# A two-layer decoder trunk on one core: the router's stage in quarters of a tile, the last expert batch in halves

## The chip, the cores and the metric

One Trainium2 chip, one of its cores. The metric is device time in microseconds (us) of one execution, lower is better. Everything is float32. The engines are PE (TensorE), DVE (VectorE), ACT (ScalarE), POOL (GpSimd) and SP (SyncE, which here only issues DMAs); each runs its own instructions in order, and they meet in semaphores.

## What is computed

Two layers (`DEPTH`), 256 tokens, width 1024. Each layer has a token mixer (three kinds of attention over one input projection, then one output projection) and a mixture of experts, each followed by a LayerNorm over `ALPHA * x + sublayer(x)`. The part that the change touches, cut from the reference:

```python
o = jnp.concatenate([o_a, o_b, o_c], axis=1).transpose(0, 2, 1, 3).reshape(B, S, MIX_W)
return o @ w_out                       # the mixer's output projection
# then x = layer_norm(ALPHA * x + that)

s = jax.nn.sigmoid((xf @ router_w).astype(jnp.float32))      # 64 experts in 8 groups
sb = (s + router_b).reshape(T, N_GROUPS, EXP_PER_GROUP)
g_sel = jnp.argmax(lax.top_k(sb, 2)[0].sum(-1), axis=-1)     # top-1 group
_, j = lax.top_k(in_grp, TOP_K)                              # top-2 experts of it
# for each block of tokens of an expert e, with its gates:
hb = jax.nn.silu(xb @ w1[e]) * (xb @ w3[e])                  # 1024 -> 256
return hb @ w2[e]                                            # 256 -> 1024
```

All 64 experts of a layer are read, 3 MiB each (`w1`, `w3`, `w2`), 192 MiB in a layer.

## The kernel before, in words

Tokens stand in two tiles of 128 (t = 0, 1). A layer runs in three stages.

**Mixer.** SP streams `w_in`, PE projects, attends pair by pair, and ends with `out_chunk(t, h, c)` (line 672): tile t, column half h (512 columns), chunk c of 8. Eight chunks make a half of a tile; `mix_psum` counts the halves.

**Router stage.** DVE's `add_mix(t, h)` (line 1141) adds the residual into x and takes the statistics; PE turns the result chunk by chunk (`transpose_z`, line 570), ACT copies it to `xT`, PE multiplies by the router (`route`, line 794; `z_psum`), DVE computes the scores and the choice (`scores`, `select`, lines 1174 and 1189; `picked`), PE counts ranks (`rank`), DVE places (`place`, line 1215), and PE gathers the first batch's rows (`gather_first`, line 840) in two banks. DVE scales its first four chunks into `xg` (line 1277), ACT the other four (line 1513). While this runs the normalised rows x are finished: tile 0 by DVE (`center_first`, then `stretch`, `x0_ready`), tile 1 by POOL in four instructions (lines 519 and 523, `x1_ready`), which start when `routed` is up. PE's order is written out by hand in lines 810 to 862, DVE's in 1244 to 1282, ACT's in 1500 to 1515.

**Experts in batches.** A batch is four experts (k = 0 to 3) of 32 rows each, 16 batches in a round. `batch` (line 876) multiplies `w1` and `w3` (line 890, `part_psum` once for each k), folds four partial sums (897), has DVE compute silu times up (1304 to 1307) from ACT's exponential, turns the hidden rows (912), copies them to `hT` (DVE, 1311), multiplies by `w2` (`down`, line 919; `y2_psum`) and adds the rows to Y (927). Before its k = 2 product PE waits for DVE's copy of k = 0 (line 885), and DVE reaches that copy (1294) only after all of its router stage, `start_batches` (line 1282, a load of the batch count into a register) and `choose`. Between the projections of a batch PE gathers the rows of the next (871).

**Weights.** There are two sets of slots, even and odd. The two first batches are loaded during the mixer. SP issues batch 2's `w1` and `w3` of expert k when batch 0's `part_psum` k is up (`load_first`, line 415), then, when x0 and x1 are ready, one matrix that is still missing of batch 1 (`load_w2(1, 3, 1)`, line 430), then batch 2's four `w2` when batch 0's `y2_psum` is up (431). All later ones follow the same rule, two batches back. The last batch's `w2` come as eight column halves: four first halves (`w2_first_in`), then four second ones (448 to 453). In the last batch the first halves are multiplied for all k (932), the second ones k by k (937); `keep_warm` products fill some waits.

Of the kernel before, what the change touches and what calls it, by code (L numbers as in the profile page):

```python
# [79 lines left out]
def program(nc, a, consts, const_at, out):  # L80
# [17 lines left out]
    with ctx:  # L98
# [129 lines left out]
        class Signal:  # L228
# [23 lines left out]
        xT_psum, xT_dve, xT_act = Signal("xT_psum", 8), Signal("xT_dve", 3), Signal("xT_act", 7)  # L252
# [10 lines left out]
        mix_psum = Signal("mix_psum", 4)  # L263
# [5 lines left out]
            Signal("z_ready", 4), Signal("n_ready", 2), Signal("y_bits_set", 4), Signal("y_seeded", 4))  # L269
# [4 lines left out]
        chosen_ok, xg_dve, xg_act = Signal("chosen_ok"), Signal("xg_dve"), Signal("xg_act")  # L274
        gathered = Signal("gathered_first_half"), Signal("gathered_second_half")
# [9 lines left out]
        w2_first_in = Signal("w2_last_first_half_in", NB * 16)  # L285

        shift_ok, n2_ready = Signal("n2_shift_ok", 2), Signal("n2_ready", 4)
        out_dve, out_pool = Signal("out_dve"), Signal("out_pool")
        y2_first, y_half = Signal("y2_last_first_half_psum", 1), Signal("y_first_half_added", 2)
# [33 lines left out]
        def _(sp):  # L323
# [3 lines left out]
            for l in range(DEPTH):  # L327
# [27 lines left out]
                if l == 0:  # L355
# [26 lines left out]
                sp.dma_start(router.rearrange("p (h c) e -> p h (c e)", h=2),  # L382
                             a["router_w"].rearrange("(h p c) e -> p h (c e)", h=2, c=4)).then_inc(router_in.sem, 16)
                sp.dma_start(router_bias, a["router_b"].partition_broadcast(P)).then_inc(router_in.sem, 16)
                for v, name in enumerate(("ln1_g", "ln1_b")):
                    sp.dma_start(g_cols[:, v, :], a[name].rearrange("l (p c) -> l p c", c=DC)[l]).then_inc(cols_in.sem, 16)
                    sp.dma_start(r_cols[:, v, :].rearrange("p (h c) -> p h c", h=2),
                                 a[name].rearrange("l (h p c) -> l p h c", h=2, c=4)[l]).then_inc(cols_in.sem, 16)
# [19 lines left out]
                after(sp, l, mix_psum, 4)  # L408
# [57 lines left out]
        def _(pool):  # L466
# [5 lines left out]
            for l in range(DEPTH):  # L472
# [40 lines left out]
                after(pool, l, xT_psum, 8)  # L513
# [24 lines left out]
        def _(pe):  # L538
# [16 lines left out]
            for l in range(DEPTH):  # L555
# [14 lines left out]
                def transpose_z(t, h):  # L570

                    after(pe, l, z_ready, 2 * t + h + 1)
                    zc = x[:, t, h * 512:(h + 1) * 512].rearrange("p (d c) -> p c d", c=4)
                    for c in range(4):
                        last = nc.tensor.transpose(bank[2 * t + h][:, c * P:(c + 1) * P], zc[:, c, :], ident)
                    last.then_inc(xT_psum.sem, 1)

# [216 lines left out]
                def route(t, h):  # L794
                    after(pe, l, xT_act, 3 + 2 * t + h + 1)
                    if t == 1 and h == 0:
                        after(pe, l, z_lin, 1)
                    for c in range(4 * h, 4 * h + 4):
                        last = mm(bank[0][:, t * NE:(t + 1) * NE], xT[:, c, t * P:(t + 1) * P], router[:, c, :],
                                  start=c == 0, stop=c == DC - 1)  # L800
                    if h == 1:
# [10 lines left out]
                transpose_z(0, 0)  # L812
                transpose_z(0, 1)
# [16 lines left out]
                out_chunk(1, 1, 5)  # L830
                out_chunk(1, 1, 6)
                out_chunk(1, 1, 7)
                route(1, 0)
                set_bits(0, 0)
                transpose_z(1, 1)

                set_bits(0, 1)
                route(1, 1)

                def gather_first(t):  # L840
                    nc_ = nrm[t].rearrange("p (d c) -> p c d", c=DC)
                    for c in range(DC):
                        last = mm(bank[2 + c // 4][:, c % 4 * P:(c % 4 + 1) * P], nc_[:, c, :], chosen[:, t, :],
                                  start=t == 0 and c % 4 == 0, stop=t == 1, skip_group_check=True)
                        if t == 1 and c % 4 == 3:
                            last.then_inc(gathered[c // 4].sem, 1)
# [29 lines left out]
                def batch(j, parity, last_of_all):  # L876
# [32 lines left out]
                    pe.wait_ge(hn_ok.sem, b + 1)  # L909
                    hc = hn.rearrange("p (f c) -> p c f", c=2)  # L910
                    for c in range(2):
                        last = nc.tensor.transpose(bank[1][:, SEQ + c * P:SEQ + (c + 1) * P], hc[:, c, :], ident)  # L912
                    last.then_inc(hT_psum.sem, 1)
                    pe.wait_ge(hT_sb.sem, b + 1)
# [4 lines left out]
                    def down(h):  # L919
                        for c in range(2):  # L920
                            for k in range(NB):
                                last = mm(bank[2 + h][BLK * k:BLK * (k + 1), :], hT[:, c, BLK * k:BLK * (k + 1)],  # L922
                                          w2_slots[parity][k][:, c, h * 512:(h + 1) * 512], start=c == 0, stop=c == 1)
# [6 lines left out]
                    if last_of_all:  # L930
                        after(pe, l, w2_first_in, NB * 16)
                        down(0).then_inc(y2_first.sem, 1)
# [7 lines left out]
                    else:  # L940
                        for k in range(NB):
                            pe.wait_ge(w2_in[parity][k].sem, (b0 + j) * 8 + 16)
                        down(0)
# [614 lines left out]
```

## Time and profile before

| | us |
|---|---|
| median of 3 runs (lowest to highest) | 1198.57 (1197.81 to 1199.47) |
| the profiled execution, own time | 1198.07 |
| its span in the trace | 1196.1 |
| PE busy / DVE / ACT / POOL | 1070.3 / 373.9 / 196.3 / 34.0 |
| bytes moved by DMA | 442.68 MB, mean 370 GB/s |

The profiled execution is 0.5 us below the median, and 1.97 us of its time lie outside the span. The profile page cuts the span in 40 slices of 29.9 us; the row of GB/s shows when the core's DMA engines are full (420) and when they are not. The timeline gives for each group of instructions its start, the time from its first start to its last end, engine, line, operation, operands, count, and in brackets how long the engine had stood idle and who released it. PE shows twice as many matmuls as the code calls, since a float32 product is two passes.

### The profile page before, as it was taken

Reading aid. Unit: us, or ns where it says so; the run is one execution under the profiler, and the core shown is the slowest. Engines: PE = TensorE matmul, PEld = TensorE weight load, DVE = VectorE, ACT = ScalarE, POOL = GpSimd, SP = SyncE. Lnnn points to the kernel's source line nnn. Section 1 sums busy time; section 2 is a strip of 40 time slices with the busy share of each in tenths; the row PEclk is TensorE's granted clock in tenths of the full one; section 3 lists DMA queues with packets and bytes.
Section 4 is the critical chain, followed back from the end, with each engine's and each line's share of the span. In section 5 each row is a group of like instructions: output and inputs, shape, how many; then the busy total and the mean of one; then the engine's idle time right before and its main releaser. Section 6 shows DMA issues by size and latency. Waiting matters only on the chain.

```text
span 1196.1 us, 16270 instructions
## 1 busy us (share of the span) xinstructions
PE 1070.3 (89%) x6084; PEld 594.7 (50%) x6088; DVE 373.9 (31%) x1007; ACT 196.3 (16%) x469; POOL 34.0 (3%) x46
## 2 busy tenths in 40 slices
PE   8999988899899888888899999899899889888885
PEld 5565555444455444444356656544455444444442
DVE  2244462222232222122251535422232222222224
ACT  1144121111111111011122441211111111100110
POOL 0010020000000000000000100100000000000001
PEclk9999999999999999989999999999999999998998
DMA  9966389999999999999998456899999999999996
GB/s 353 345 222 246 141 322 420 420 420 420 421 421 421 420 421 421 421 420 420 396 350 319 149 216 245 338 418 421 421 421 421 421 421 420 420 420 421 421 420 235
DMA packets 85026, 442.68 MB, mean 370 GB/s; under 512 B 11009, under 2 KB 26497, under 8 KB 36865
## 3 DMA queue, kind: packets, MB, share of 16 engines
q1 hardware_dynamic: 84704, 441.60, 91.3%
q0 software_dynamic: 144, 0.58, 0.1%
q8 instruction: 20, 0.33, 0.1%
q14 instruction: 14, 0.11, 0.0%
q10 hardware_dynamic: 144, 0.07, 0.0%
HBM read 441.16 MB, written 1.05 MB: 370 GB/s over the span
## 4 chain that ended last, share of the span: by engine, by line
PE 47%; SPq 35%; DMA 8%; DVE 4%; issue 3%; ACT 1%; DVEq 0%; POOL 0%
SPq L344 24%; PE bank L602 12%; SPq L348 11%; PE bank L871 8%; PE bank L890 7%; DMA w_odd<-in_moe_w 7%; PE bank L680 5%; PE bank L922 4%; PE bank L927 4%; DMA w_odd<-in_w_in 2%; PE bank L897 1%; ACT moe L1366 1%; PE bank L650 1%; PE bank L665 1%; DVE moe L1320 1%
## 5 line engine op out<-in xcount | busy, mean ns | idle before, releaser
L871 PE MATMUL bank<-moe,x 128*128 128x128 f32 x960 | 233.1, 402 | 0.0
L871 PEld LDWEIGHTS bank<-moe,x 128*128 128x128 f32 x960 | 230.8, 335 | 0.0
L1366 ACT ACTIVATE moe<-bank 128x512 f32<-128x512 f32 (+2 forms) x190 | 101.4, 543 | 750.1 <-PE bank L890 361.0
L602 PE MATMUL bank<-w_odd 128*128 128x384 f32 (+1 forms) x448 | 150.9, 493 | 4.8 <-DMA w_odd<-in_w_in 2.9
L927 PE MATMUL bank<-moe 128*128 128x512 f32 x256 | 118.4, 605 | 24.1 <-DVE moe L1320 24.1
L890 PE MATMUL bank<-w_even,moe 128*32 128x512 f32 x1024 | 118.7, 609 | 17.1 <-DMA w_even<-in_moe_w 13.1
L890 PE MATMUL bank<-w_odd,moe 128*32 128x512 f32 x1024 | 118.0, 606 | 14.0 <-DMA w_odd<-in_moe_w 14.0
L1294 DVE COPY moe<-bank 128x512 f32<-128x512 f32 x64 | 44.2, 691 | 248.4 <-PE bank L890 248.1
L602 PEld LDWEIGHTS bank<-w_odd 128*128 128x128 f32 x448 | 83.6, 190 | 63.6 <-issue 14.2
L927 PEld LDWEIGHTS bank<-moe 128*128 128x128 f32 x256 | 46.0, 190 | 98.9 <-DVE moe L1320 51.4
L890 PEld LDWEIGHTS bank<-w_even,moe 128*32 128x32 f32 x1024 | 30.9, 111 | 100.0 <-issue 72.2
L890 PEld LDWEIGHTS bank<-w_odd,moe 128*32 128x32 f32 x1024 | 31.0, 111 | 95.7 <-issue 75.7
L922 PE MATMUL bank<-w_even,moe 128*32 128x512 f32 x512 | 58.3, 594 | 14.0 <-DVE moe L1311 14.0
L922 PE MATMUL bank<-w_odd,moe 128*32 128x512 f32 x480 | 54.8, 595 | 9.6 <-DVE moe L1311 9.6
L897 PE MATMUL bank<-moe,constants 128*32 128x512 f32 x256 | 35.8, 629 | 25.8 <-ACT moe L1366 25.8
L680 PE MATMUL bank<-w_odd 128*128 128x512 f32 x128 | 58.4, 599 | 0.0
L1305 DVE RECIPROCAL moe<-moe 128x256 f32<-128x256 f32 x32 | 56.1, 1753 | 1.1
L1320 DVE COPY moe<-bank 128x512 f32<-128x512 f32 x32 | 22.1, 692 | 109.3 <-PE bank L922 109.3
L1304 DVE TENSOR_SCALAR moe<-moe 128x256 f32<-128x256 f32 x32 | 9.4, 294 | 142.8 <-ACT moe L1525 142.8
L1366 ACT ACTIVATE w_odd<-bank 128x384 f32<-128x384 f32 (+3 forms) x74 | 32.5, 472 | 119.9 <-PE bank L602 34.5
L1311 DVE COPY moe<-bank 128x256 f32<-128x256 f32 x32 | 13.6, 425 | 101.6 <-PE bank L912 101.6
L922 PEld LDWEIGHTS bank<-w_even,moe 128*32 128x32 f32 x512 | 18.1, 109 | 42.7 <-issue 42.7
(160 smaller groups left out, 684.6 us busy)
## 6 DMA issues: line engine op xcount, KB each, us to landing
w_even<-in_moe_w SPq DMA_DIRECT2D x192, 1024.0 KB, 26.1
w_odd<-in_moe_w SPq DMA_DIRECT2D x184, 1024.0 KB, 26.4
w_odd<-in_w_in SPq DMA_DIRECT2D x24, 768.0 KB, 6.4
w_odd<-in_w_out SPq DMA_DIRECT2D x4, 2048.0 KB, 10.3
w_odd<-in_moe_w SPq DMA_DIRECT2D x16, 512.0 KB, 16.8
w_odd<-in_w_in SPq DMA_DIRECT2D x4, 832.0 KB, 10.9
w_odd<-in_ln_g SPq DMA_DIRECT2D x4, 512.0 KB, 7.9
w_odd<-in_ln_b SPq DMA_DIRECT2D x4, 512.0 KB, 8.7
```

The lines of the kernel that those rows point to most:

```text
L344: sp.dma_start(w13_slots[parity][k][:, m, :, :].rearrange("p c f -> p (c f)"), w[l * NE + e * NB + k]).then_inc(w13_in[parity][k].sem, 16)
L348: sp.dma_start(w2_slots[parity][k].rearrange("p c d -> p (c d)"), w2[l * NE + e * NB + k]).then_inc(w2_in[parity][k].sem, 16)
L602: last = mm(h_bank[b][t][:, 0:n], xT[:, c, t * P:(t + 1) * P], w[:, c, :], start=c == 0, stop=c == DC - 1)
L680: last = mm(mix_bank[t][h][:, :], oT[:, c, t * P:(t + 1) * P], w_out_half[h][:, c, :], start=c == 0, stop=c == DC - 1, skip_group_check=True)
L871: last = mm(bank[2 + c // 4][:, c % 4 * P:(c % 4 + 1) * P], xc[:, t, c, :], chosen[:, t, :], start=t == 0, stop=t == 1)
L890: last = mm(bank[k % 2][BLK * q:BLK * (q + 1), :], xg[:, c, BLK * k:BLK * (k + 1)], w[:, :, c, :], start=c < 4, stop=c >= 4)
L897: last = mm(bank[0][BLK * k:BLK * (k + 1), :], const("fold"), partial[:, k, :], start=True, stop=True)
L922: last = mm(bank[2 + h][BLK * k:BLK * (k + 1), :], hT[:, c, BLK * k:BLK * (k + 1)], w2_slots[parity][k][:, c, h * 512:(h + 1) * 512], star ...
L927: return mm(Y[t][h][:, :], scatter[:, t * P:(t + 1) * P], y_rows[:, h * 512:(h + 1) * 512], start=False, stop=True, skip_group_check=True)
L1294: nc.vector.tensor_copy(partial[:, k, :], bank[k % 2][:, :]).then_inc(part_dve.sem, 1)
L1305: blink(nc.vector.reciprocal(eg, eg))
L1366: return fn(dst, src, ACT.Copy)
```

## The change

Router stage. The last output half of tile 1 is made as two quarters of 256 columns (`out_quarter(2, c)` into bank 3, `out_quarter(3, c)` into bank 6), with their own add, statistics, transposes (two instead of four), copy and router products; `mix_psum`, `z_ready`, `xT_psum` and `xT_act` count one more. The router's rows and its scales are loaded in quarters. DVE no longer runs `center_first` between these steps: half 0 stands where `stretch` half 0 stood, half 1 ahead of the gathered rows, and both halves of `stretch` behind them. `gather_first` puts chunks 4 and 5 into bank 3 (`first_mid`, scaled by ACT) and chunks 6 and 7 into bank 1 (scaled by DVE). POOL starts on tile 1's rows at `rows_go`, behind DVE's chunk 6, not at `routed`. ACT seeds Y only behind its two chunks.

Last batch of each layer. DVE's four instructions of the activation run on the even hidden columns, then on the odd ones; PE turns and multiplies the first half (`down(0, 0)`) before the second is turned; ACT copies the first turned half. The `w2` of k = 0 and 1 come whole, then the first halves of k = 2 and 3, then their second halves. Cut to its core:

```diff
-                route(0, 0)
-                route(0, 1)
+                route(0, range(4), 4)
+                route(0, range(4, DC), 5)
                 out_chunk(1, 0, 7)
-                for c in range(5):
-                    out_chunk(1, 1, c)
-                transpose_z(1, 0)
+                for c in range(DC):
+                    out_quarter(2, c)
+                transpose_half(1, 0)
+                out_quarter(3, 0)
                 rank = bank[1]
                 after(pe, l, picked, 1)
                 mm(rank[:, 0:NE], const("before"), key[:, 0, :], start=True, stop=True,
...
-                out_chunk(1, 1, 5)
-                out_chunk(1, 1, 6)
-                out_chunk(1, 1, 7)
-                route(1, 0)
+                for c in range(1, 5):
+                    out_quarter(3, c)
+                transpose_quarter(2)
+                for c in range(5, DC):
+                    out_quarter(3, c)
+                route(1, range(4), 6)
+                route(1, (4, 5), 7)
                 set_bits(0, 0)
-                transpose_z(1, 1)
-
+                transpose_quarter(3)
                 set_bits(0, 1)
-                route(1, 1)
+                route(1, (6, 7), 8)
...
-                center_first(0)
-                link(add_mix(1, 1))
-                moments(1, 5, LN_EPS)
-                center_first(1)
+                link(add_quarter(2))
+                link(add_quarter(3))
+                moments(1, 5, LN_EPS, 3)
                 scores(1)
                 select(1)
-                stretch(0, 0, x0_ready, (0,))
+                center_first(0)
...
                 weigh_scores(1)
-                stretch(0, 0, x0_ready, (1,))
+                center_first(1)
...
                 last.then_inc(xg_dve.sem, 1)
+                v.wait_ge(gathered[1].sem, b0 + 1)
+                after(v, l, first_mid_sb, 1)
+                for c, sig in ((6, rows_go), (7, xg_act)):
+                    ts(xg[:, c, :], bank[1][:, (c - 4) * P:(c - 3) * P], g_cols[:, 0, c:c + 1], g_cols[:, 1, c:c + 1],
+                       ALU.mult, ALU.add).then_inc(sig.sem, 1)
+                stretch(0, 0, x0_ready)
                 weights(1)
...
-                after(pool, l, routed, 1)
+                after(pool, l, rows_go, 1)
...
+                for k in range(2):
+                    load_w2(BATCHES - 1, k, 1)
                 for h in range(2):
-                    for k in range(NB):
+                    for k in range(2, NB):
...
                     if last_of_all:
-                        after(pe, l, w2_first_in, NB * 16)
-                        down(0).then_inc(y2_first.sem, 1)
+                        for k in range(2):
+                            pe.wait_ge(w2_in[parity][k].sem, (b0 + j) * 8 + 16)
+                        after(pe, l, w2_first_in, 2 * 16)
+                        after(pe, l, hT_half_sb, 1)
+                        down(0, 0)
+                        pe.wait_ge(hn_ok.sem, b + 1)
+                        turn_hidden(1).then_inc(hT_psum.sem, 1)
+                        pe.wait_ge(hT_sb.sem, b + 1)
+                        down(0, 1).then_inc(y2_first.sem, 1)
```

## Rows read from the trace of the kernel before

**Rows 1.** Page: data rate in 40 slices of the span
```profile
GB/s 353 345 222 246 141 322 420 420 420 420 421 421 421 420 421 421 421 420 420 396 350 319 149 216 245 338 418 421 421 421 421 421 421 420 420 420 421 421 420 235
```
**Rows 2.** Timeline, SP queue, first batches of layers 0 and 1: start, us
```profile
164.80 7.97 SPq L344 DMA_DIRECT2D w_even<-in_moe_w  x8
...
186.54 1.75 SPq L348 DMA_DIRECT2D w_even<-in_moe_w  x4
...
754.57 7.50 SPq L344 DMA_DIRECT2D w_even<-in_moe_w  x8
...
775.88 1.75 SPq L348 DMA_DIRECT2D w_even<-in_moe_w  x4
```
**Rows 3.** Windows: busy of five engines, PE clock, DMA share, GB/s
```profile
167.00:168.00 1.00, 0.00 (x0) 0.00 (x0) 0.86 (x3) 0.05 (x1) 0.00 (x0) 1.00 1.00 418
```
**Rows 4.** Timeline of PE, layer 0, router stage: start, us
```profile
139.93 5.37 PE L680 MATMUL bank<-w_odd 128*128 128x512 f32 x12
145.14 0.74 PE L575 MATMUL bank<-constants,x 128*128 128x128 f32 x4
146.11 2.79 PE L680 MATMUL bank<-w_odd 128*128 128x512 f32 x6
151.19 1.10 PE L799 MATMUL bank<-moe,w_odd 128*128 128x64 f32 x8 [0.47 <-ACT w_odd L1366]
```
**Rows 5.** Timeline of DVE, layer 0, router stage
```profile
147.67 0.25 DVE L1207 TENSOR_SCALAR moe<-moe,small 128x64 f32<-128x64 f32 x1
...
149.01 0.69 DVE L1144 SCALAR_TENSOR_TENSOR x<-x,bank 128x512 f32<-128x512 f32 x1 [0.29 <-PE bank L680]
...
152.39 0.28 DVE L1179 SCALAR_TENSOR_TENSOR moe<-bank,small 128x64 f32<-128x64 f32 x1
...
156.56 0.75 DVE L1165 SCALAR_TENSOR_TENSOR x<-x,small,w_odd 128x512 f32<-128x512 f32 x1
```
**Rows 6.** Timeline of PE, layer 0, first gather and batch 0
```profile
157.83 4.18 PE L843 MATMUL bank<-moe 128*128 128x128 f32 x16 [0.36 <-DVE moe L1212]
162.37 4.02 PE L890 MATMUL bank<-w_even,moe 128*32 128x512 f32 x32 [0.36 <-DVE moe L1277]
168.19 3.64 PE L890 MATMUL bank<-w_even,moe 128*32 128x512 f32 x32 [1.80 <-DVE moe L1294]
```
**Rows 7.** Timeline of DVE and POOL, layer 0, into batch 0
```profile
158.86 2.95 POOL L519 TENSOR_TENSOR x<-moe,w_odd 128x512 f32<-128x512 f32 x2 [6.88 <-DVE iters L1271]
158.98 1.69 DVE L1165 SCALAR_TENSOR_TENSOR x<-x,small,w_odd 128x512 f32<-128x512 f32 x1
160.60 1.35 DVE L1277 TENSOR_SCALAR moe<-bank,small 128x128 f32<-128x128 f32 x4
161.89 2.50 POOL L523 TENSOR_TENSOR x<-x,w_odd 128x512 f32<-128x512 f32 x2
...
163.25 1.50 DVE L1233 TENSOR_TENSOR moe<-moe 128x128 f32<-128x128 f32 x2
...
166.81 0.49 DVE L1212 TENSOR_TENSOR moe<-constants,moe 128x128 f32<-128x128 f32 x2 [1.99 <-issue]
```
**Rows 8.** PE after a long wait for a weight: timeline, then its clock
```profile
490.36 3.51 PE L890 MATMUL bank<-w_even,moe 128*32 128x512 f32 x16 [2.98 <-DMA w_even<-in_moe_w]
...
490.00:491.00 1.00, 0.64 (x4) 0.20 (x8) 0.00 (x0) 0.00 (x0) 0.00 (x0) 0.59 1.03 426
```
**Rows 9.** Last batch, layer 1: chain, a window, timeline
```profile
1142.09 27.75 DMA w_odd<-in_moe_w
...
1170.00:1172.00 2.00, 1.80 (x16) 0.30 (x13) 0.00 (x0) 0.13 (x1) 0.00 (x0) 1.00 1.04 386
...
1174.48 1.75 DVE L1305 RECIPROCAL moe<-moe 128x256 f32<-128x256 f32 x1
...
1178.28 1.92 PE L922 MATMUL bank<-w_odd,moe 128*32 128x512 f32 x16 [0.52 <-DVE moe L1311]
...
1180.02 2.58 PE L937 MATMUL bank<-w_odd,moe 128*32 128x512 f32 x16
```

More of the change, by code:

```diff
@@ L407, in _ @@
                 load_w13(1, 1, 1)
-                after(sp, l, mix_psum, 4)
+                after(sp, l, mix_psum, 5)
                 load_w13(1, 0, 1)
@@ L792, in _, with out_quarter, route @@
                 out_chunk(0, 1, 7)
-                def route(t, h):
-                    after(pe, l, xT_act, 3 + 2 * t + h + 1)
-                    if t == 1 and h == 0:
+                def out_quarter(q, c):
+                    last = mm((bank[3], bank[6])[q - 2][:, 0:256], oT[:, c, P:2 * P],
+                              w_out_half[1][:, c, (q - 2) * 256:(q - 1) * 256],
+                              start=c == 0, stop=c == DC - 1, skip_group_check=True)
+                    if c == DC - 1:
+                        last.then_inc(mix_psum.sem, 1)
+                def route(t, chunks, copied):
+                    after(pe, l, xT_act, copied)
+                    if t == 1 and chunks[0] == 0:
                         after(pe, l, z_lin, 1)
-                    for c in range(4 * h, 4 * h + 4):
+                    for c in chunks:
                         last = mm(bank[0][:, t * NE:(t + 1) * NE], xT[:, c, t * P:(t + 1) * P], router[:, c, :],
                                   start=c == 0, stop=c == DC - 1)
-                    if h == 1:
+                    if c == DC - 1:
                         last.then_inc(z_psum.sem, 1)
@@ L842, in gather_first @@
                     for c in range(DC):
[L843 to L846, printed above, removed]
+                        to, o = (bank[2], c * P) if c < 4 else (bank[3], (c - 4) * P) if c < 6 else (rank, (c - 4) * P)
+                        last = mm(to[:, o:o + P], nc_[:, c, :], chosen[:, t, :],
+                                  start=t == 0 and c in (0, 4), stop=t == 1, skip_group_check=True)
+                        if t == 1 and c in (3, 5, 7):
+                            last.then_inc((gathered[0] if c == 3 else first_mid if c == 5 else gathered[1]).sem, 1)
                 after(pe, l, n_ready, 1)
@@ L917, in batch, with down @@
                         pe.wait_ge(xg_act.sem, b + 2)
[L919 to L923, printed above, removed]
+                    def down(h, c):
+                        for k in range(NB):
+                            last = mm(bank[2 + h][BLK * k:BLK * (k + 1), :], hT[:, c, BLK * k:BLK * (k + 1)],
+                                      w2_slots[parity][k][:, c, h * 512:(h + 1) * 512], start=c == 0, stop=c == 1)
                         return last
@@ L942, in batch @@
                             pe.wait_ge(w2_in[parity][k].sem, (b0 + j) * 8 + 16)
-                        down(0)
-                        down(1).then_inc(y2_psum.sem, 1)
+                        down(0, 0)
+                        down(0, 1)
+                        down(1, 0)
+                        down(1, 1).then_inc(y2_psum.sem, 1)
                     pe.wait_ge(y2_dve.sem, b + 1)
@@ L1499, in _ @@
                 copy_xT(0, 0, 5)
+                copy_xT(0, 1, 6)
                 route(0)
                 copy_xT(1, 0, 7)
+                for q in (2, 3):
+                    after(act, l, xT_psum, 6 + q)
+                    copy(xT[:, 2 * q:2 * q + 2, P:2 * P],
+                         (bank[3], bank[7])[q - 2][:, 0:256].rearrange("p (c t) -> p c t", c=2)).then_inc(xT_act.sem, 1)
                 route(1)
                 m, b0 = start_batches(act, base, l)
-                seed(0)
                 def copy_gathered(g):
@@ L1510, in _ @@
                 after(act, l, cols_in, 96)
-                act.wait_ge(gathered[1].sem, b0 + 1)
-                for c in range(4):
+                after(act, l, first_mid, 1)
+                for c in range(2):
                     last = fn(xg[:, 4 + c, :], bank[3][:, c * P:(c + 1) * P], ACT.Identity,
                               scale=g_cols[:, 0, 4 + c:5 + c], bias=g_cols[:, 1, 4 + c:5 + c])
-                last.then_inc(xg_act.sem, 1)
+                last.then_inc(first_mid_sb.sem, 1)
+                seed(0)
                 seed(1)
```

106 lines of the change are left out of this document (72 added, 34 removed).

## The prediction, on record before the changed kernel ran

> **What bounds the kernel now.** The page's row of data rates comes first: each layer has a dozen slices in a row at 420 GB/s and a dip ahead of them [rows 1]. Over most of a layer the time is bytes at a fixed rate. An edit shows where it moves the start of that stretch, opens a hole in it, or changes what follows the last weight. Next come SP's issues. The stretch starts with the issue behind batch 0's first `part_psum`, at 164.80 and 754.57 [rows 2]; at 167.0 the rate is full [rows 3]. Until batch 0's `y2_psum` SP can issue 8 MiB of `w1`/`w3` and one left `w2`, 9.44 MB, 22.5 us at 420 GB/s. Its next issue comes 186.54 - 164.80 = 21.7 us behind the first in layer 0 and 775.88 - 754.57 = 21.3 in layer 1 [rows 2]. The same lag from issue to data lies at both ends, so the engines would run dry only 0.7 and 1.2 us later. Two times therefore count in the first batch: when `part_psum` 0 comes, and whether `y2_psum` comes within 22.5 us of it. A delay of the second beyond the slack is added to the layer whole. Last I read the timeline from the mixer's end to batch 0, and the tail behind the last weight.
>
> **Front, PE's order.** Product of 512 columns: 2.79 / 6 = 0.43 us a pass, less a drain of 0.2; a pass of 256 I take at half, 0.213 (bounds 0.19 and 0.30), so a quarter costs 16 x 0.213 = 3.4. Chunk (1, 0, 7) starts at 139.93 [rows 4] and ends at 140.8; the first quarter ends at 144.2. Now `transpose_half(1, 0)` waits for DVE's add, as before at 145.14 [rows 4]: PE idles 0.9 where it had column half 1 to do. It goes on at about 145.7, does one chunk (0.43) and then the rank products, which before gave way to the next product at 146.11 [rows 4]; now they end at 146.55. DVE's placing and weights end 0.43 later too, 147.92 [rows 5] + 0.43 = 148.35, and the add of quarter 2 (between 0.28 for 64 columns and 0.69 for 512 [rows 5], some 0.42) is done at 148.8. PE has finished chunk 4 of quarter 3 at 148.2 and waits for it in `transpose_quarter(2)`, with the last three chunks queued behind. Those start at 149.15. Before, DVE's last add started 149.01 - 146.11 = 2.9 behind six passes of 0.43 [rows 4, 5]; now it starts 1.28 + 0.34 behind 149.15, at 150.8, **1.8 later**.
>
> What follows the last add is shorter, but less than it looks. Before: 152.39 - 149.01 = 3.4 to the scores [rows 5]. Now the add (0.42) is hidden: PE is busy from 150.4 with twelve router passes at 1.10 / 8 = 0.14 with their drain, 0.12 without [rows 4], and `set_bits`, until 152.1. Then two transposes (0.74 for four [rows 4], so 0.45), ACT's copy of 256 columns (0.4, estimate from DVE's 0.28 and 0.69), four router passes (0.6) and the handovers: the scores start at 153.8. That is **+1.4**. The choice takes 156.56 - 152.39 = 4.2 as before [rows 5]. `center_first` (0.75, like `stretch` [rows 5]) takes the place of `stretch` ahead of `place(1)`, but its `link` lets it drain: +0.1. The second gather starts 1.5 later, bounds 0 and 2.2. The three weight loads that follow `mix_psum` and `z_psum` move with it; batch 1 needs them, some 25 us later, so they cost nothing. The smaller DMAs of router rows and scales lie far ahead and cost nothing.
>
> **Front, first rows.** I count from the gather's start g (157.83 before [rows 6]). PE starts batch 0 at g + 4.5 in both, behind its own gather and the register load. Its products of k = 0 and 1 took 4.02 where two others take 3.64 [rows 6]: 0.4 waited for ACT's four chunks. Two for ACT and two for DVE end 0.8 earlier: -0.4. So `part_psum` 0 comes 1.5 - 0.4 = **1.1 later**.
>
> **Front, DVE's way to its first copy.** This is the largest term. The copy of k = 0 gates PE's k = 2, and PE already waited 1.80 for it, starting at 168.19 = g + 10.4 [rows 6]. Queued on DVE ahead of it now, behind the first four chunks (which end at g + 3.5): the wait for the whole gather and chunks 6 and 7, each 1.35 / 4 [rows 7], to g + 4.9; both halves of `stretch`; weights; gates; the register load 1.99; `choose`, handover and copy, 168.19 - 166.81 = 1.4 [rows 6, 7]. POOL's four instructions (2.95 + 2.50 [rows 7]) no longer lie beside DVE's gathered chunks, they start at g + 4.7 and lie beside all this. `stretch` takes 0.75 alone [rows 5] and 1.69 beside POOL [rows 7], weights 1.3 and gates 1.5 beside it [rows 7], about half alone. Contended: 4.9 + 3.4 + 1.3 + 1.1 (POOL ends within the gates) + 2.0 + 1.4 = g + 14.1, the copy being late by 3.7. Alone: 4.9 + 1.5 + 0.7 + 0.7 + 2.0 + 1.4 = g + 11.2, late by 0.8. I take 3.6, since rows 7 are the same instructions beside the same POOL work. On ACT the seeds wait for the same rows and are ready earlier than DVE.
>
> The Trainium skill has a rule on this pair (page "SBUF — State Buffer", section "Who interferes with whom"): a DVE instruction with two SBUF inputs and a GpSimd instruction that reads SBUF exclude each other, and the second to start blocks until the first has finished. By it a `stretch` that starts 0.12 behind a POOL instruction of 1.47 would take 2.1; the trace shows 1.69, so it agrees in kind and not in size. With 2.1 for both the sum would be 0.8 a layer higher, 1211.6.
>
> PE then idles from g + 8.2 to g + 14, some 5.8 us. Elsewhere a wait of 2.98 left it at a granted clock of 0.59 in the next microsecond, that is at 1.2 of 2.4 GHz, and sixteen products took 3.51 [rows 8] where thirty-two take 3.64 [rows 6]: +1.7 for one such fall. I add 1.6 here (0 if it stays up, 3.6 if k = 2 and 3 run wholly at the low level).
>
> Sum for `y2_psum`: 1.5 + 3.6 + 1.6 = 6.7 later. Less the slack of 0.7 and 1.2: **+6.0 and +5.5**. PE then needs fewer microseconds a batch than the weights, so no second hole opens, and nothing gives it back.
>
> **Tail.** The last `w3` is seen at 1142.09 + 27.75 = 1169.84 [rows 9]. Halves of w2 flow at 386 GB/s [rows 9], whole ones should at 420: 2 MiB whole, 1 MiB in halves, 5.0 + 2.7, so the first halves are complete at 1177.5; the last at 1180.6 or 0.4 earlier, ahead of PE's last k either way. Activation by halves: each about 1.9 (reciprocal 0.9, half of 1.75 [rows 9]; three others 0.3), the first turned and copied at 1176.8. So `down(0, 0)` waits for the weights to 1177.5, not for DVE; 0.86 for four products, then a turn (0.4), copy (0.3) and 0.86 for `down(0, 1)`: the second halves start at 1180.0, where they start now at 1180.02 [rows 9]. **0**, bounds -0.6 (weights early) and +0.5. The shorter chain of DVE is covered by transfers; if that cover went, 0.6 a layer would appear.
>
> **Total.** 1198.07 + 6.0 + 5.5 + 0 = 1209.6 by the profiled execution; the median stands 0.5 above it: **1210**.
>
> **Rivals.** (a) As above, but PE's clock stays up: 2 x 1.6 less, 1206.9. For it: shorter waits pass without a fall, as that of 1.80 ahead of k = 2 [rows 6]. (b) DVE and POOL do not slow each other: copy late by 0.8, `y2_psum` by 2.3, less slack 1.6 + 1.1, 1201.3. Rows 7 speak against it. (c) The backlog is deeper than 9.44 MB at 420 makes it, and the late copy is hidden: only `part_psum` counts, 2 x 1.1, 1200.8. (d) **Faster:** quarter 2's add comes in time, so that quarter 3 ends when half 1 did; the scores start 1.4 earlier (add, turn, copy and router products of 256 columns for 512), the first chunks 0.4 earlier, and POOL moved away leaves DVE's copy in its old place in time: 2 x 1.8 less, 1195.0. It decides where PE reaches `transpose_quarter(2)` behind DVE's add, and DVE's copy within 0.7 of its old distance. Against it: DVE reaches that add only through `place(0)` and the weights. (e) The front balances out and the halves do nothing, as under Tail: 1198.6.
>
> **Chances.** Forecast 0.40, (a) 0.15, (b) 0.14, (c) 0.10, (d) 0.15, (e) 0.06. Within 0.2%, 2.4 us, which is about what a measurement of this kernel can tell from no change, lie (c), (e): 0.16. Slower: 0.69. Faster: 0.15. The range reaches from (e) to the forecast with the clock low throughout k = 2 and 3: 1198 to 1213.5; the forecast's own range is 1207 to 1213.5.
>
> **What would show it.** In the changed profile: DVE's add of quarter 3 near 150.8; scores near 153.8; `part_psum` 0, seen as SP's first issue, near 165.9; PE's k = 2 some 14 behind the second gather's start; `y2_psum` some 27 behind the first issue; a window of a few us below 420 GB/s near 190; in the last batch PE waiting for w2 ahead of `down(0, 0)`. I am wrong if the two first-batch distances are no longer than now, or if the gap in the data rate is missing.

## The result, and the profile after

| | before | after |
|---|---|---|
| median, us (runs made together) | 1199.02 (4) | 1211.62 (4), 1210.46 to 1212.43 |
| ratio, 95% interval | | 1.0102, 1.0083 to 1.0120 |
| profiled execution, its span | 1198.07, 1196.1 | 1211.48, 1209.5 |

The change makes the kernel 12.6 us slower by the medians, 13.4 by the two profiled spans. The forecast was 1210.0, with 1207 to 1213.5 as its own range.

The page of after, data rate in 40 slices, to be laid beside [rows 1]: the dip ahead of the long stretch at 421 is longer in both layers, and the stretch itself runs at the same rate (a slice is 30.2 us here, 29.9 before).

```profile
GB/s 351 341 218 244 139 309 367 420 421 421 421 421 421 421 421 421 421 420 420 402 345 322 153 198 239 329 356 421 421 421 421 421 421 421 421 421 421 421 418 242
```

The timeline of SP's queue, after (start, us, engine, line, operation). It answers to [rows 2].

```profile
165.99 14.31 SPq L349 DMA_DIRECT2D w_even<-in_moe_w  x8
...
194.06 1.95 SPq L353 DMA_DIRECT2D w_even<-in_moe_w  x4
...
762.86 14.02 SPq L349 DMA_DIRECT2D w_even<-in_moe_w  x8
...
790.64 2.00 SPq L353 DMA_DIRECT2D w_even<-in_moe_w  x4
```

From `part_psum` 0 to `y2_psum` it is now 28.07 and 27.78 us, as SP's two issues show, where it was 21.7 and 21.3. That is past the 22.5 us of transfers that SP can have issued by then. The windows of after (busy time of PE, its weight loads, DVE, ACT, POOL; granted clock; DMA share; GB/s) show the engines run dry:

```profile
177.00:178.00 1.00, 1.00 (x12) 0.31 (x8) 0.41 (x1) 0.00 (x0) 0.00 (x0) 0.70 0.52 213
178.00:179.00 1.00, 1.00 (x16) 0.12 (x6) 0.28 (x1) 0.00 (x0) 0.00 (x0) 1.00 0.42 82
179.00:180.00 1.00, 0.34 (x4) 0.00 (x0) 0.00 (x0) 0.58 (x1) 0.00 (x0) 1.00 0.81 229
...
191.00:192.00 1.00, 1.00 (x12) 0.31 (x8) 0.00 (x0) 0.00 (x0) 0.00 (x0) 1.00 0.58 238
192.00:193.00 1.00, 1.00 (x16) 0.44 (x12) 0.00 (x0) 0.00 (x0) 0.00 (x0) 1.00 0.02 8
193.00:194.00 1.00, 0.94 (x12) 0.03 (x3) 0.00 (x1) 0.01 (x1) 0.00 (x0) 1.00 0.00 0
194.00:195.00 1.00, 0.26 (x1) 0.26 (x2) 1.00 (x3) 0.59 (x1) 0.00 (x0) 1.00 0.00 0
195.00:196.00 1.00, 1.00 (x3) 0.42 (x3) 0.18 (x1) 0.00 (x0) 0.00 (x0) 1.00 0.69 172
```

There are two holes, not one. In the windows just ahead of them and behind them the rate is 418 to 451. Against 420 KB in each microsecond the first lacks 207 + 338 + 191 = 736 KB, the second 182 + 412 + 420 + 420 + 248 = 1682 KB: 1.8 and 4.0 us of transfer, 5.8 together, where 28.07 - 22.5 = 5.6 were to be expected. The first hole comes because SP issues k = 2 and 3 of batch 2 only behind `part_psum` 2, and PE waits ahead of that product:

```profile
159.40 4.18 PE L873 MATMUL bank<-moe 128*128 128x128 f32 x16 [0.59 <-DVE moe L1262]
...
163.94 3.64 PE L920 MATMUL bank<-w_even,moe 128*32 128x512 f32 x32
173.88 5.47 PE L920 MATMUL bank<-w_even,moe 128*32 128x512 f32 x32 [6.30 <-DVE moe L1349]
...
755.84 4.17 PE L873 MATMUL bank<-moe 128*128 128x128 f32 x16 [0.93 <-DVE moe L1262]
...
769.72 6.21 PE L920 MATMUL bank<-w_even,moe 128*32 128x512 f32 x32 [5.28 <-DVE moe L1349]
```

That is the timeline of PE, after, in both layers; the bracket is PE's idle time and who ended it. Before, the same wait in layer 0 was 1.80 and the 32 passes behind it took 3.64 [rows 6]. Layer 1 before, the same timeline:

```profile
747.53 4.17 PE L843 MATMUL bank<-moe 128*128 128x128 f32 x16 [0.37 <-DVE moe L1212]
752.07 4.09 PE L890 MATMUL bank<-w_even,moe 128*32 128x512 f32 x32 [0.36 <-DVE moe L1277]
757.49 3.64 PE L890 MATMUL bank<-w_even,moe 128*32 128x512 f32 x32 [1.34 <-DVE moe L1294]
```

What DVE did meanwhile in layer 0, and POOL beside it, is in their timelines of after:

```profile
163.64 0.73 DVE L1332 TENSOR_SCALAR moe<-bank,small 128x128 f32<-128x128 f32 x2 [0.46 <-PE bank L873]
164.28 3.46 DVE L1215 SCALAR_TENSOR_TENSOR x<-x,small,w_odd 128x512 f32<-128x512 f32 x2
...
168.10 0.81 DVE L1257 TENSOR_SCALAR moe<-moe,small 128x64 f32<-128x64 f32 x1
168.94 1.49 DVE L1283 TENSOR_TENSOR moe<-moe 128x128 f32<-128x128 f32 x2
...
172.50 0.49 DVE L1262 TENSOR_TENSOR moe<-constants,moe 128x128 f32<-128x128 f32 x2 [1.99 <-issue]
173.13 0.69 DVE L1349 COPY moe<-bank 128x512 f32<-128x512 f32 x1
...
164.22 2.98 POOL L527 TENSOR_TENSOR x<-moe,w_odd 128x512 f32<-128x512 f32 x2 [11.36 <-DVE moe L1332]
167.27 2.81 POOL L531 TENSOR_TENSOR x<-x,w_odd 128x512 f32<-128x512 f32 x2
```

Both halves of `stretch` lie beside POOL's first pair, the gates beside its second, and the copy on which PE waits is last in the queue. PE's granted clock from 171 to 177 is 0.50, the low level. Before, the last `w3` products of the two layers started at 580.17 and 1169.88, after at 586.91 and 1183.45: 6.74 later, then 13.57.

### The profile page after: what moved, and what is told of

It is laid out like the page before. It is cut to its first block, busy times and chain, and to the rows that moved or that the text cites. A ratio compares the mean times of both kernels' runs of the same rounds, so it can differ in the third digit from the quotient of the medians.

```text
span 1209.5 us, 16348 instructions
## 1 busy us (share of the span) xinstructions
PE 1074.7 (89%) x6120; PEld 600.8 (50%) x6120; DVE 378.7 (31%) x1023; ACT 196.1 (16%) x469; POOL 33.5 (3%) x46
## 4 chain that ended last, share of the span: by engine, by line
PE 46%; SPq 38%; DMA 6%; DVE 5%; issue 3%; ACT 1%; DVEq 0%; POOL 0%; ACTq 0%
SPq L349 24%; SPq L353 13%; PE bank L620 12%; PE bank L901 8%; PE bank L920 7%; DMA w_odd<-in_moe_w 4%; PE bank L958 4%; PE bank L963 3%; PE bank L698 3%; DMA w_odd<-in_w_in 2%; PE bank L927 1%; PE bank L668 1%; PE bank L683 1%; ACT moe L1442 1%; DVE x L1215 1%
## 5 line engine op out<-in xcount | busy, mean ns | idle before, releaser
L920 PE MATMUL bank<-w_even,moe 128*32 128x512 f32 x1024 | 123.1, 629 | 23.9 <-DMA w_even<-in_moe_w 12.3
L620 PEld LDWEIGHTS bank<-w_odd 128*128 128x128 f32 x448 | 83.5, 190 | 63.1 <-issue 14.2
L958 PE MATMUL bank<-w_even,moe 128*32 128x512 f32 x512 | 58.2, 594 | 13.9 <-DVE moe L1388 13.9
L1364 DVE RECIPROCAL moe<-moe 128x256 f32<-128x256 f32 (+1 forms) x34 | 56.4, 1658 | 1.2
L1363 DVE TENSOR_SCALAR moe<-moe 128x256 f32<-128x256 f32 (+1 forms) x34 | 9.7, 286 | 142.6 <-ACT moe L1605 142.6
L698 PE MATMUL bank<-w_odd 128*128 128x512 f32 x96 | 44.2, 600 | 0.0
```

The source lines that it names most:

```text
L620: last = mm(h_bank[b][t][:, 0:n], xT[:, c, t * P:(t + 1) * P], w[:, c, :], start=c == 0, stop=c == DC - 1)
L698: last = mm(mix_bank[t][h][:, :], oT[:, c, t * P:(t + 1) * P], w_out_half[h][:, c, :], start=c == 0, stop=c == DC - 1, skip_group_check=True)
L920: last = mm(bank[k % 2][BLK * q:BLK * (q + 1), :], xg[:, c, BLK * k:BLK * (k + 1)], w[:, :, c, :], start=c < 4, stop=c >= 4)
L1364: step(nc.vector.reciprocal(e, e))
```

## Experiments

**One part of the change at a time.** Four kernels split it: the kernel before with only the last batch's new order; the changed kernel with the last batch as before; the quarters alone; the first rows alone (gather in three parts, `stretch` behind them, POOL at `rows_go`).

Last batch alone, in the kernel before:

```diff
+                for k in range(2):
+                    load_w2(BATCHES - 1, k, 1)
                 for h in range(2):
-                    for k in range(NB):
+                    for k in range(2, NB):
```

with DVE's, PE's and ACT's halves.

> The kernel before with only the last batch changed (activation by halves, two down matrices whole and two by halves); the router's stage is that of before. Theory: the changed kernel's last batch ends 0.2 us earlier behind its last w3 than before, in both layers (from the last w3 product to the first row product 12.43 and 12.45 instead of 12.64 and 12.65), since the first down product waits for weights: 2 x -0.2, so 1198.2 to 1199.0, no difference that can be told. Rival: the last batch carries a part of the loss, 2 us or more: above 1201.

Measured: 1198.85 against 1198.93, ratio 0.9999 (0.9989 to 1.0009). The halves make no difference that the medians can tell; what the traces show of them, 0.2 us a layer, stands under the tail below.

The front alone, the changed kernel with the last batch as it was:

```diff
-                for k in range(2):
-                    load_w2(BATCHES - 1, k, 1)
                 for h in range(2):
-                    for k in range(2, NB):
+                    for k in range(NB):
```

> The changed kernel with the last batch of before. Theory: the whole loss is in the front: +13.0, so 1211.5 to 1213, SP's two first-batch issues some 28 us apart as in the changed kernel. Rival: some of the loss was in the tail: under 1209.

Measured: 1212.64, ratio 1.0125 (1.0108 to 1.0142). The whole loss is in the front. (The 1.0 above the changed kernel's median is within what the two intervals leave open.)

The quarters alone:

```diff
-                for c in range(5):
-                    out_chunk(1, 1, c)
-                transpose_z(1, 0)
+                for c in range(DC):
+                    out_quarter(2, c)
+                transpose_half(1, 0)
+                out_quarter(3, 0)
```

> Of the front only the quarters of the last output half, with their adds, transposes, copies and router products; the two centering steps lie in DVE's two idle stretches there, and the first gather, stretch, POOL's start and ACT's seeds are as before. Theory: the second gather starts 1.4 to 1.6 later in each layer (with the distance from SP's first issue to its next unchanged at 21.7 and 21.3), so +3.0 in all: 1201.5. Rival 1, the quarters carry the loss: 1208 or more. Rival 2, they save time as meant and the other edits lose it: 1196.

Measured: 1202.04, ratio 1.0028 (1.0016 to 1.0041). The second gather starts at 159.07, 1.24 later, and SP's distance is as before (21.5 and 21.1): a later start costs one for one, and the distance stays under 22.5.

The first rows alone:

```diff
+                for c, sig in ((6, rows_go), (7, xg_act)):
+                    ts(xg[:, c, :], bank[1][:, (c - 4) * P:(c - 3) * P], ...).then_inc(sig.sem, 1)
+                stretch(0, 0, x0_ready)
                 weights(1)
...
-                after(pool, l, routed, 1)
+                after(pool, l, rows_go, 1)
```

> Of the front only the first rows: gather in three banks, two chunks by ACT and two by DVE, stretch behind them, POOL started behind chunk 6. The output half is made whole and centered as before. Theory: DVE's first copy comes 3.6 to 4 later behind the gather, PE's clock falls in the wait, the distance between SP's two issues is 27 to 28; first issue 0.4 earlier; y2_psum 5.5 to 6 later, less the slack 0.7 and 1.2: +4.9 and +4.7, 1208.5. Rival: if the delay is hidden by the backlog: -0.8, 1198.

Measured: 1208.17, ratio 1.0076 (1.0059 to 1.0093). Its PE timeline has the same two long waits, ahead of products at the low clock:

```profile
172.17 6.46 PE L892 MATMUL bank<-w_even,moe 128*32 128x512 f32 x32 [6.50 <-DVE moe L1300]
...
767.35 5.83 PE L892 MATMUL bank<-w_even,moe 128*32 128x512 f32 x32 [5.66 <-DVE moe L1300]
```

So about 9.2 of the loss is DVE's order and POOL's place, 3.1 the quarters; together they give 12.3 of the 12.6.

**Do DVE and POOL slow each other?** The changed kernel with POOL back at `routed`, one line:

```diff
-                after(pool, l, rows_go, 1)
+                after(pool, l, routed, 1)
```

> The changed kernel, POOL's start on tile 1's rows back at routed instead of behind DVE's chunk 6; nothing else. Theory: POOL is done some 6.6 behind the gather's start, so only the first of the two stretch steps (1.7) lies beside it, the second (0.75), the weights and the gates run alone: DVE's first copy 2.4 earlier in each layer, y2_psum 2.4 earlier or more if PE's clock stays up, in all -4.8, 1206.8; the distance between SP's two issues 25.5. Rival: the queue on DVE alone makes the delay and POOL takes no part in it: 1211.6 as the changed kernel.

Measured: 1205.65, ratio 1.0061 (1.0043 to 1.0079), 6.0 below the changed kernel. Its timeline of DVE has the same instructions without their neighbour:

```profile
164.27 2.67 DVE L1215 SCALAR_TENSOR_TENSOR x<-x,small,w_odd 128x512 f32<-128x512 f32 x2
...
167.30 0.25 DVE L1257 TENSOR_SCALAR moe<-moe,small 128x64 f32<-128x64 f32 x1
167.59 0.49 DVE L1283 TENSOR_TENSOR moe<-moe 128x128 f32<-128x128 f32 x2
```

Weights' last instruction 0.25 for 0.81, gates 0.49 for 1.49, `stretch` 2.67 for 3.46 (half of it still lies beside POOL). DVE's copy comes 2.35 earlier (170.78). POOL's place carries 6.0 of the 9.2 above. In layer 1 PE's wait falls to 2.54 and its clock stays up:

```profile
765.73 3.64 PE L920 MATMUL bank<-w_even,moe 128*32 128x512 f32 x32 [2.54 <-DVE moe L1349]
```

**The clock.** Dummy products of the identity in PE's wait ahead of k = 2, first twenty, then twelve in each even batch (the loop's body is shared, so they cannot stand in batch 0 alone):

```diff
                         w = w13_slots[parity][k]
+                        if k == 2 and parity == 0:
+                            keep_warm(20)
                         if k >= 2:
```

> The changed kernel with 20 small dummy products on PE (4.7 us) ahead of k = 2 in even batches, where PE waits for DVE's first copy. Theory: the clock stays at its upper level, the two products sets of k = 2 and 3 take 3.7 instead of 5.5 and 6.2, y2_psum comes 1.8 and 2.5 earlier, -4.3 in all, 1207.3. Rival: PE's clock has no part, since other waits cover it: 1211.6. If the dummies delay later batches it is slower than that.

Measured: 1239.55, ratio 1.0331 (1.0316 to 1.0346). Its PE timeline in batch 0:

```profile
166.71 4.73 PE L556 MATMUL bank<-constants 128*128 128x128 f32 x40
173.39 3.64 PE L922 MATMUL bank<-w_even,moe 128*32 128x512 f32 x32 [1.95 <-DVE moe L1351]
```

Here k = 2 and 3 run at the high clock, and `y2_psum` comes 26.6 behind the first issue instead of 28.1: the clock's term in layer 0 is real, 1.5 to 1.8 us. In layer 1 the 32 passes also take 3.64 and the distance is 25.3 instead of 27.8, 2.5 less. But the run is 28 us slower than the changed kernel, so PE had less in reserve than the dummies took. The next run has twelve:

```diff
-                            keep_warm(20)
+                            keep_warm(12)
```

> The changed kernel with 12 dummy products of the identity (2.84 us by the 4.73 us of the twenty) ahead of k = 2 in each even batch, less than PE's slack over the weights. Theory (the low clock behind PE's wait for the late copy is a term of its own, 1.8 us in layer 0 and 2.6 in layer 1, and PE's catching up is what the twenty cost): the wait that is left in layer 1 is 5.3 - 2.8 = 2.5, the length of the one that left the clock up in the run with POOL early, so layer 1's k = 2 and 3 take 3.64 and its y2_psum comes some 2 earlier, a distance of 25.5 to 26; in layer 0 the wait left is 3.5 and the clock may still fall. PE ends batch 14 before the last w3 is in, so nothing is lost at the layer's end: 1209.0 to 1210.5, that is 1 to 2.5 below the changed kernel's 1211.6. Rival (a dummy costs the weights' stream in itself, PE's slack is not the reason for the 28 us): 2.84 / 4.73 of them again, 1227.

Measured: 1219.46, ratio 1.0162 (1.0142 to 1.0182). Both theories missed it. The clock fell in both layers:

```profile
173.82 5.34 PE L922 MATMUL bank<-w_even,moe 128*32 128x512 f32 x32 [3.44 <-DVE moe L1351]
...
773.73 5.34 PE L922 MATMUL bank<-w_even,moe 128*32 128x512 f32 x32 [2.78 <-DVE moe L1351]
```

and PE became the bound: from batch 1 at 198 to the last `w3` product at 591 it waits for no weight, while the data rate stays at 416 to 424 GB/s in every ten us from 200 to 580. In the changed kernel PE catches up with the weights only at 462 us, and from there on waits; its timeline:

```profile
462.29 1.92 PE L920 MATMUL bank<-w_odd,moe 128*32 128x512 f32 x16 [0.42 <-DMA w_odd<-in_moe_w]
467.21 3.17 PE L920 MATMUL bank<-w_odd,moe 128*32 128x512 f32 x16 [2.99 <-DMA w_odd<-in_moe_w]
...
497.13 2.38 PE L920 MATMUL bank<-w_even,moe 128*32 128x512 f32 x16 [2.64 <-DMA w_even<-in_moe_w]
...
527.07 1.92 PE L920 MATMUL bank<-w_odd,moe 128*32 128x512 f32 x16 [2.20 <-DMA w_odd<-in_moe_w]
...
552.07 1.92 PE L920 MATMUL bank<-w_even,moe 128*32 128x512 f32 x16 [0.67 <-DMA w_even<-in_moe_w]
556.99 3.34 PE L920 MATMUL bank<-w_even,moe 128*32 128x512 f32 x16 [2.99 <-DMA w_even<-in_moe_w]
...
586.91 1.92 PE L920 MATMUL bank<-w_odd,moe 128*32 128x512 f32 x16 [0.66 <-DMA w_odd<-in_moe_w]
```

These waits are 12.6 us, and 1.6 of dummy products stand ahead of the last: 14.2 us are PE's reserve for a whole layer, or 17.3 with the 3.1 by which the products behind three of the waits exceed 1.92. In batches 2 to 14 the dummies cost 7 x 2.94 = 20.6 with twelve and 7 x 4.73 = 33.1 with twenty; those in batch 0 lie in a wait, and PE begins batch 1 there 0.2 and 2.3 earlier than in the changed kernel (198.18 and 196.05 for 198.38). So the last `w3` product of layer 0 should start 3.1 to 6.2 later with twelve and 13.5 to 16.6 with twenty. It starts at 591.36 and 603.37, 4.4 and 16.5 behind 586.91. Both lie inside. The price of the dummies was PE's time, not the stream's.

**Versions that keep the start.** (i) The quarters, with PE's order packed: all of quarter 2, the rank products, tile 1's first transposes, all of quarter 3, quarter 3's transposes between the router products, and `set_bits` last. On DVE it is as in the quarters alone, against which the diff stands:

```diff
-                transpose_half(1, 0)
-                out_quarter(3, 0)
                 rank = bank[1]
...
-                for c in range(1, 5):
+                transpose_half(1, 0)
+                for c in range(DC):
                     out_quarter(3, c)
                 transpose_quarter(2)
-                for c in range(5, DC):
-                    out_quarter(3, c)
-                route(1, range(4), 6)
+                route(1, (0, 1), 6)
+                transpose_quarter(3)
+                route(1, (2, 3), 6)
```

> The kernel with the quarters alone (front otherwise as before, 1202.0), with PE's order repacked: the rank products in the wait ahead of tile 1's first transposes, quarter 3 in one piece, quarter 2's transposes behind it, quarter 3's transposes behind the first two router chunks. Theory: the 1.2 to 1.4 a layer that quarters cost are PE's two waits and its order, not the quarters: scores 0.3 to 0.4 earlier than in the kernel before, 1198.3. Rival: the cost is in the quarters themselves (more instructions, shorter products, more handovers): 1201 or more.

Measured: 1198.54, ratio 0.9993 (0.9984 to 1.0002). The second gather starts at 157.44, 1.6 ahead of the quarters as changed: what the quarters lost is PE's order, not the width of 256. Against the kernel before hardly anything is gained. The 0.4 to [rows 6] holds 0.2 of an earlier mixer (tile 0's router products start at 137.97, before at 138.20); counted from those products, the gather is 0.16 sooner in layer 0 and 0.06 later in layer 1.

(ii) The gather in three parts, but one half of `stretch` ahead of the gathered chunks, DVE's register load ahead of them too, POOL at `routed`, and the new last batch. Against the kernel before:

```diff
                 weigh_scores(1)
-                stretch(0, 0, x0_ready, (1,))
+                m, b0 = start_batches(v, base, l)
...
+                stretch(0, 0, x0_ready, (1,))
                 weights(1)
                 weigh(0, b0)
-                m, b0 = start_batches(v, base, l)
+                plain(v)
```

> The kernel before with the changed last batch, with the gather in three banks, two chunks by ACT and two by DVE, but POOL started at routed as before, only the second half of stretch behind the gathered chunks, and DVE's load of the batch count ahead of them, where DVE waits for the gather anyway. Theory: SP's first issue 0.4 earlier in each layer, its next 0.8 earlier, no hole in the data rate; with the tail -1.2 in all, 1197.8. Rival: stretch behind the chunks is what costs, wherever the load stands: DVE's copy later than before, a hole, 1202 or more.

Measured: 1198.61, ratio 0.9994 (0.9985 to 1.0003). SP's first issues come at 163.91 and 754.18, 0.9 and 0.4 earlier than before. The expected "no hole" holds in layer 1 only. In layer 0 PE's clock fell behind a wait of 1.99 (5.34 for the 32 passes), SP's next issue came at 187.53, 23.6 behind the first, and the 0.9 was lost again.

(iii) Both together:

> The packed quarters, the register load ahead of the gathered chunks with the first gather in three parts and half of the stretch behind it, and the last batch's new order, all in one. Theory (the times of the first issue and of y2_psum add up, and the weights' stream turns them into time one for one): gather near 157.4, first issues near 163.5 and 753.8, y2_psum near 187.1 and 775.5, so 0.2 of layer 0 and 0.8 of layer 1 below the kernel before, and 0.4 from the two tails: 1197.6, ratio 0.9988. Rival (what the front gains is given back in the mixer or in the wait for weights, as each of the two parts alone came out at 0.9993 and 0.9994): 1198.6, ratio 0.9995 to 1.0000.

Measured: 1198.23 against 1199.00, ratio 0.9990 (0.998 to 1.000, 12 runs and 17). Its SP timeline in layer 1:

```profile
753.76 7.63 SPq L348 DMA_DIRECT2D w_even<-in_moe_w  x8
...
775.16 1.75 SPq L352 DMA_DIRECT2D w_even<-in_moe_w  x4
```

In layer 0 nothing was gained: the issues come at 165.23 and 186.54, the first 0.4 later than before, since PE reached tile 0's router products 0.6 later in this execution (138.81 for 138.20). The median is the lowest of all, 0.1% below the kernel before, and that is at the edge of what the interval can tell.

**All of them by one rule.** In layer 1 SP has work out for 22.5 us from its first issue F. The stream goes on from the later of F + 22.5 and Y, `y2_psum`'s issue. Before, that is 754.57 + 22.5 = 777.07. What each kernel moves this by, with the 0.2 that the new last batch saves, against what its span did (1196.1 before):

| kernel | F | Y | moved by | span by |
|---|---|---|---|---|
| changed | 762.86 | 790.64 | 13.57 - 0.2 = 13.4 | 13.4 |
| front alone | 762.78 | 790.06 | 13.0 | 13.2 |
| first rows alone | 760.11 | 787.92 | 10.9 | 10.9 |
| POOL at `routed` | 761.62 | 784.08 | 7.05 - 0.2 = 6.9 | 7.0 |
| quarters alone | 757.51 | 778.64 | 2.9 | 2.9 |
| last batch alone | 757.05 | 778.00 | 2.5 - 0.2 = 2.3 | 2.4 |
| quarters packed | 754.62 | 775.42 | 0.05 | 0.2 |
| version (ii) | 754.18 | 775.90 | -0.4 - 0.2 = -0.6 | -0.6 |
| version (iii) | 753.76 | 775.16 | -0.8 - 0.2 = -1.0 | -1.1 |
| twelve dummies | 766.49 | 793.80 | 16.7 - 0.2 = 16.5 | 20.8 |

F and Y are times from the start of the span, so they hold what layer 0 did. Layer 0 by itself passes the same test: there the later of F + 22.5 and Y moves from 187.30 to 194.06 in the changed kernel, by 6.76, and the last `w3` product by 6.74; in the other eight rows ahead of the dummies the two agree within 0.15 us. Nine spans fall within 0.2 us of the rule. The last does not, and there PE no longer waits for weights. The twenty dummies, left out of the table, are another such case. (In the profiled execution of the last batch alone the 2.5 come from the mixer of layer 0, which the edit does not touch; the medians show no difference.)

## Why the prediction was right, step by step

**The bound** held: bytes at a fixed rate, moved by two times of the first batch. The table is its test. The order on PE, the queue on DVE and POOL's place enter through F and Y alone. In the new order no further hole opened behind the first batch, as forecast: 417 to 424 GB/s in every ten us from 200 to 580.

**PE's order**: the last add was forecast for 150.8 and the scores for 153.8. After's timeline of DVE:

```profile
150.88 0.42 DVE L1188 SCALAR_TENSOR_TENSOR x<-x,bank 128x256 f32<-128x256 f32 x1 [1.51 <-PE bank L813]
...
153.74 0.28 DVE L1229 SCALAR_TENSOR_TENSOR moe<-bank,small 128x64 f32<-128x64 f32 x1 [0.64 <-PE bank L824]
```

The second gather moved by 1.57 (1.5 forecast), SP's first issue by 1.19 (1.1) to 165.99. In layer 1, where 6.5 is carried over from layer 0, the gather moved by 755.84 - 747.53 - 6.5 = 1.8, and the issue by 762.86 - 754.57 - 6.5 = 1.8: there k = 0 and 1 took 4.07, as 4.09 before, so the 0.4 for ACT's chunks was gained in layer 0 only. In layer 1 the clock took it: the granted clock from 760 to 761, as those passes begin, is 0.50. In the front alone it is 1.00 there, and they took 3.64.

**DVE's way to the copy** was forecast as g + 14.1 and is g + 14.48 in layer 0, g + 13.88 in layer 1. Term by term in layer 0: chunks to g + 4.88 (4.9), `stretch` 3.38 (3.4), weights 1.28 (1.3), gates 1.57 (1.1), register load 1.99 (2.0), the rest 1.38 (1.4). The gates are the term that was mis-sized: POOL was taken to end within them, its two pairs at their old 2.95 + 2.50; they took 2.98 + 2.81, ended at 170.08 and lay beside nearly all of the gates. In layer 1 the way was shorter than forecast, by the register load (1.40 for 2.0). But the sum had taken the old way from layer 0 (g + 10.4), and in layer 1 it had been g + 9.96 (757.49 - 747.53), so the copy's delay was 3.92 there and not 3.6.

By the Trainium skill's rule (page "SBUF — State Buffer", section "Who interferes with whom") each half of `stretch` would have taken 2.1 and the time, by the prediction's estimate, 1211.6. The median equals that figure, but not for that reason: the two took 3.46 together, 1.73 each, as [rows 7] had it. The trace agrees with the rule that DVE and POOL hold each other up (the run with POOL at `routed`), not with a full block.

**The clock** fell, as forecast, and cost more: 5.47 - 3.64 = 1.83 in layer 0 and 6.21 - 3.64 = 2.57 in layer 1, where 1.6 stood, inside its bounds of 0 and 3.6. Rival (a) falls by these rows, and rival (b) by the run with POOL at `routed`. Rival (c), a deeper backlog, falls by the holes: 5.8 us of them are what a backlog of 22.5 leaves. Rival (e), a front that balances out, falls by the front alone, 13 us slower than before.

**The sum** for `y2_psum` was 6.7. In layer 0 it is 1.57 + 4.12 + 1.83 = 7.52 (194.06 - 186.54), in layer 1 1.81 + 3.92 + 2.57 = 8.30 (8.26 by SP). Less the slack, 6.8 and 7.1 were lost, not 6.0 and 5.5. Of the 2.4 between, 1.2 is the clock, 0.8 the copy's delay, 0.4 the gather. The forecast of 1210.0 is 1.6 below the median because of them, less the 0.4 that the two tails gave. All three came out larger than forecast; only the tails went the other way.

**The hole near 190** came, as a second one behind a first that the text had not seen. It cost nothing of its own: what SP has issued by `y2_psum` is 9.44 MB in any order, so two holes take what one would.

**The tail** was forecast at 0 and is -0.2: from the last `w3` product to the first row product 12.65 before and 12.44 after (1195.89 - 1183.45), 12.64 and 12.43 in layer 0. `down(0, 0)` does wait for the weights, which are seen 7.68 behind that product (7.7 forecast). The timeline of PE, after:

```profile
1191.37 1.07 PE L958 MATMUL bank<-w_odd,moe 128*32 128x512 f32 x8 [0.97 <-DMA w_odd<-in_moe_w]
...
1193.14 1.06 PE L958 MATMUL bank<-w_odd,moe 128*32 128x512 f32 x8 [0.38 <-DVE moe L1386]
1194.02 1.94 PE L980 MATMUL bank<-w_odd,moe 128*32 128x512 f32 x16
```

Wrong was "ahead of PE's last k either way". The second halves took 2.58 before [rows 9] and 1.94 now, while they start 0.43 later. The 0.64 of difference was a wait for the last weights, which stood in [rows 9] as a duration and was read as work. No bracket shows it; PE's weight loads do: before, the last of them stands 1.56 behind the second group (1181.58 and 1180.02), after 0.86 (1194.88 and 1194.02).

**Rival (d)**, faster, failed at the point that it named: quarter 3 ended late behind `transpose_quarter(2)`, and DVE's copy left its place. The packed order takes that loss back, but not the 1.4 of the rival: its gather stands 0.2 sooner than before in one layer and as before in the other. Its timeline of DVE in layer 0 shows why:

```profile
149.19 0.42 DVE L1164 SCALAR_TENSOR_TENSOR x<-x,bank 128x256 f32<-128x256 f32 x1 [0.35 <-PE bank L807]
...
151.76 0.21 DVE L1202 TENSOR_SCALAR small<-small 128x1 f32<-128x1 f32 x1 [0.51 <-POOL small L477]
152.01 0.28 DVE L1205 SCALAR_TENSOR_TENSOR moe<-bank,small 128x64 f32<-128x64 f32 x1
```

The last add starts 0.2 later than before, and the scores stand 2.82 behind it instead of 3.4. What ends last ahead of them is POOL's step on the variance, not the router products, so of the shorter steps only the add and the statistics count (0.42 + 0.43 for 0.69 + 0.69).

## What to carry to other kernels

Where a stream of weights is the bound, look for the two times that gate its start, the first release and the one that must come before what has been issued is used up: within the cover between them a delay is free, past it every microsecond counts, in each layer. Work that nobody needs soon (here `stretch` and POOL's rows) belongs neither in the queue ahead of a copy that another engine waits for nor beside a second engine that slows it: 1.5 us of it took 3.4, the small instructions behind it took three times their time, and the wait that came of it cost clock as well. Before filling a wait in a shared loop body, add up what the engine has in reserve over the whole loop.

## What was not expected of the hardware

**The clock does not go by the wait's length alone.** PE's waits ahead of k = 2, and the 32 passes behind them (3.64 at the high level):

| wait | passes | kernel, layer |
|---|---|---|
| 1.76, 1.80 | 3.64, 3.64 | version (ii) layer 1, before layer 0 |
| 1.95 | 3.64 | twenty dummies, 0 |
| 1.99 | 5.34 | version (ii), 0 |
| 2.54 | 3.64 | POOL at `routed`, 1 |
| 2.78, 3.44 | 5.34, 5.34 | twelve dummies, 1 and 0 |
| 4.13 | 6.23 | POOL at `routed`, 0 |
| 5.28, 6.30 | 6.21, 5.47 | changed, 1 and 0 |
| 5.66, 6.50 | 5.83, 6.46 | first rows alone, 1 and 0 |
| 5.91, 6.63 | 5.07, 6.53 | front alone, 1 and 0 |

The waits that the table leaves out, 0.70 to 1.80, left the clock up.

Waits of 1.99 (clock down) and 2.54 (clock up) stand the wrong way round, and one of 6.30 cost less than one of 4.13. A fall cost 1.4 to 2.9 us in these first batches. It does not always come within the wait: in the changed kernel the clock is 0.50 from 171 on, while PE still waits; with twelve dummies it is 1.00 to 174 and 0.53 in the next microsecond, behind the wait. Filling part of a wait with products didn't keep the clock up where 2.78 and 3.44 were left (twelve dummies), and did where 1.95 was left (twenty).

**The stall behind DVE's register load** was 1.99 in layer 0 and 1.40 in layer 1 of the same run, with "issue" as its releaser, that is, nothing that the profile shows ended it. In version (ii), where the load stands ahead of the gathered chunks, the idle time at its old place is 0.62.
